# Second block of a two-block forward pass: four units direct and 18 pairs in place of six and 17, with another order of the first pair's residues

## The chip, the cores and the metric

One core of a Trainium2 chip runs the whole kernel as one program. The metric is the device time of one execution in microseconds (us); lower is better. The kernel is written by engine: TensorE (matmuls), VectorE (DVE), ScalarE (ACT), GpSimd (POOL) and SyncE (SP, which issues loads) each run their own list of instructions in order and meet only at semaphores.

## The reference, cut to what matters

Two transformer-like blocks follow each other on one sequence of 1024 tokens of width 1024, in fp32. The first is gated linear attention with a short convolution and a gated feed-forward part. The second, in which the change lies, begins with one wide projection:

```python
h = rmsnorm_2(x, g_norm[layer])
proj = h @ w_in[layer]           # 1024 -> 9 * 1024 columns
a_u, a_v, a_gate, q, k, v, b_gate, gate_logits = jnp.split(proj, splits, axis=-1)
y_a = chunked_spatial_gating(gelu(a_u), gelu(a_v), w_s, b_s, g_v) * silu(a_gate)
y_b = dilated_attention(q, k, v) * silu(b_gate)
g_a, g_b = jnp.split(sigmoid(gate_logits), 2, axis=-1)
merged = g_a * (y_a @ w_proj_a) + g_b * (y_b @ w_proj_b)
x = x + merged @ w_out
```

The columns of q, k, v (24 tiles of 128), a_v (8 tiles) and a_u (8 tiles) are the 40 units that the change deals with.

## The kernel before, in words

**Units.** A unit is a tile of 128 output columns for all 1024 tokens, with 1024 inputs in 8 parts of 128. The sums are kept near fp32: weights and activations are each split into a high part that TensorE takes as it is and a low part, the residue, and three matmuls (high by high, low by high, high by low) are added up (lines 839 to 841). A direct unit is 2 halves of tokens x 8 parts x 3 = 48 matmuls of 512 columns. For each unit SP loads 512 KB of raw weights (line 513), ScalarE casts them to the high part (line 1289), GpSimd makes the residue in two instructions (line 727), TensorE multiplies, and VectorE takes the result out of PSUM (line 1941).

**Pairs.** Two units together are a 2 x 2 by 2 x 2 product of blocks (inputs in even and odd parts, tokens in left and right halves). `pair_of_units` computes it with seven block products instead of eight, by Winograd's form of Strassen's rule. One block product is `times`: 4 parts x 3 matmuls = 12 matmuls, so a pair is 84 matmuls where two direct units are 96. Each product needs its weights as a high part in a ring of four half buffers (`hi_half` on ScalarE, line 1455) and the residue of it (`lo_half` on GpSimd, line 767). Four of the seven weight blocks are sums (`weight_sums` on VectorE, lines 2151 to 2162). After a pair, VectorE and ScalarE join the four PSUM banks into two tiles; three VectorE additions (lines 2349 to 2354 in the second block) stand between product 3 and product 6. `half(p, i)` says which half buffer product i of pair p uses; at one pair the ring skips a buffer, so that it ends where the next stage needs it.

**Opening of the second block.** Products 0, 1 and 3 read sums of activations (x_sums_split), products 2, 4, 5 and 6 the four quarters of the activations themselves. Sums and quarters need their own high parts (`hi_sum`, `hi_again` on ScalarE, lines 1436 and 1443) and residues (`lo_sum`, `lo_again` on VectorE, lines 2131 and 2138). The quarters must be made anew, since the direct units read another scaling of the same buffer; their high parts can be written only when the last direct unit has been multiplied. All of this, eight scalings of the residual by VectorE (line 2306) and three differences (lines 2310 to 2323) happen while TensorE computes the six direct units 101 to 106 (`U_W` on). Then come the 17 pairs: q = 0 and 5 to 12 hold q, k, v tiles, 1 to 4 hold a_v, 13 to 16 hold a_u. Beside pairs 6 to 13 TensorE also transposes and mixes one a_v tile (group 0 to 7).

**What sets the order.** Nothing plans it at run time: each engine's list is written out by hand. The lines that matter are the end of the ScalarE list before the loop over q (lines 1632 to 1656), the VectorE list from `direct(0)` (line 2303) to the same loop, and `load_duo` on SP (line 545, its loads at 556), whose waits say when a raw buffer is free. There are two raw buffers for pairs: `WR`, which the direct units also use, and `WRB`, used by pairs alone (`w_pair`).

## Time and profile before

| what | value |
|---|---|
| median of 3 runs | 2347.03 us (2346.66 to 2348.51) |
| the profiled execution's own time | 2345.13 us |
| its span, first to last instruction | 2343.1 us |
| TensorE busy | 2330.0 us, 99% |
| VectorE, ScalarE, GpSimd busy | 56%, 37%, 35% |
| granted TensorE clock, mean | 0.999 |

The span is the stretch of the trace; the own time of the profiled execution is 2.0 us longer, since it also holds what lies around the first and the last instruction. All times inside the kernel are counted from the start of the span. A busy share of 99% on one engine says that the others matter only where they make it wait. In a timeline row the number after the start is the duration; instructions of one kind that follow each other closely are merged, with their count (x2) and their total.

### The profile page before, as it was taken

What the parts mean: (1) busy time and instruction counts of PE and PEld (TensorE: products, weight loads), DVE (VectorE), ACT (ScalarE), POOL (GpSimd) and SP (SyncE); (2) the same over time, 40 slices, a digit from 0 to 9 for tenths busy, and PEclk for the clock granted to TensorE, in tenths of its full rate; (3) what the DMA queues carried; (4) which work ended last, traced back from release to release, by engine and by line L of the source; (5) the groups of instructions that cost most, each with busy time, mean ns of one, the idle gap of its engine ahead of it and who ended that gap; (6) DMA issues with size and microseconds to landing.
All of it is one profiled execution on the core that took longest, in us unless ns stands there. A gap on an engine that the chain in (4) does not pass through costs nothing.

```text
span 2343.1 us, 30043 instructions
## 1 busy us (share of the span) xinstructions
PE 2330.0 (99%) x11126; PEld 1939.0 (83%) x11126; DVE 1316.8 (56%) x1830; ACT 867.8 (37%) x1309; POOL 822.2 (35%) x543
## 2 busy tenths in 40 slices
PE   9999999999999999999999999999999999999998
PEld 7888888888888888888888888888888888888887
DVE  6445764864444432247745445678787787752445
ACT  5422323233323331133443223455555555541122
POOL 3322222355555533322555455312222222223332
PEclk9999999999999999999999999999999999999999
DMA  3111222232222252223312323432332332353223
GB/s 144 43 42 37 98 82 99 81 153 81 81 81 81 81 177 93 81 99 119 116 67 74 113 98 122 156 109 91 106 125 91 97 116 81 108 189 126 108 99 117
DMA packets 70448, 238.02 MB, mean 102 GB/s; under 512 B 8432, under 2 KB 12752, under 8 KB 70224
## 3 DMA queue, kind: packets, MB, share of 16 engines
q1 hardware_dynamic: 54416, 181.20, 23.2%
q10 hardware_dynamic: 15936, 55.49, 5.9%
q8 instruction: 66, 1.08, 0.2%
q14 instruction: 30, 0.25, 0.0%
HBM read 177.41 MB, written 59.24 MB: 101 GB/s over the span
## 4 chain that ended last, share of the span: by engine, by line
PE 98%; DVE 1%; DMA 0%; issue 0%; ACT 0%; SPq 0%; DVEq 0%; ACTq 0%
PE dense L839 19%; PE dense L841 18%; PE dense L840 18%; PE dense L1030 10%; PE dense L1032 10%; PE dense L1031 10%; PE aux L1169 3%; PE aux L1182 2%; PE aux L1154 1%; PE aux L1181 1%; PE aux L1153 1%; PE aux L1116 1%; PE aux L984 1%; PE aux L863 0%; PE aux L955 0%; PE dense L1253 0%
## 5 line engine op out<-in xcount | busy, mean ns | idle before, releaser
L727 POOL TENSOR_TENSOR w_lo<-w_raw,w_hi 128x512 fp32r<-128x512 f32 x246 | 387.5, 1596 | 982.2 <-ACT w_hi L1289 973.1
L839 PE MATMUL dense<-x_hi,w_hi 128*128 128x512 f32 x1424 | 578.6, 406 | 0.4 <-DVE x_lo L1887 0.4
L841 PE MATMUL dense<-x_hi,w_lo 128*128 128x512 f32 x1424 | 557.1, 391 | 0.0
L840 PE MATMUL dense<-x_lo,w_hi 128*128 128x512 f32 x1424 | 556.7, 391 | 0.0
L1289 ACT CAST w_hi<-w_raw 128x1024 fp32r<-128x1024 f32 x121 | 127.1, 1051 | 539.8 <-PE dense L841 523.9
L841 PEld LDWEIGHTS dense<-x_hi,w_lo 128*128 128x128 f32 x1424 | 267.5, 188 | 57.7
L767 POOL TENSOR_TENSOR w_lo<-w_sums,w_hi 128x512 fp32r<-128x512 f32 x144 | 228.9, 1598 | 229.5 <-ACT w_hi L1455 229.4
L839 PEld LDWEIGHTS dense<-x_hi,w_hi 128*128 128x128 f32 x1424 | 268.2, 188 | 45.7 <-issue 1.2
L840 PEld LDWEIGHTS dense<-x_lo,w_hi 128*128 128x128 f32 x1424 | 268.7, 189 | 43.3
L1030 PE MATMUL dense<-x_hi,w_hi 128*128 128x512 f32 x576 | 226.0, 392 | 1.1 <-DVE work L2217 0.9
L1031 PE MATMUL dense<-x_lo,w_hi 128*128 128x512 f32 x576 | 224.5, 390 | 0.0
L1032 PE MATMUL dense<-x_hi,w_lo 128*128 128x512 f32 x576 | 224.5, 390 | 0.0
L1455 ACT CAST w_hi<-w_sums 128x512 fp32r<-128x512 f32 x144 | 89.1, 620 | 238.8 <-DVE w_sums L2151 169.4
L1030 PE MATMUL dense<-x_sums_split,w_hi 128*128 128x512 f32 x432 | 168.4, 390 | 0.0
L1032 PE MATMUL dense<-x_sums_split,w_lo 128*128 128x512 f32 x432 | 168.4, 390 | 0.0
L1031 PE MATMUL dense<-x_sums_split,w_hi 128*128 128x512 f32 x432 | 168.3, 390 | 0.0
L1721 ACT CAST att_p_hi<-aux 128x512 fp32r<-128x512 f32 x192 | 92.0, 479 | 144.7 <-PE aux L1169 144.4
L839 PE MATMUL dense<-work_split,w_hi 128*128 128x512 f32 x352 | 137.4, 390 | 0.7 <-DVE work_split L2167 0.6
L840 PE MATMUL dense<-work_split,w_hi 128*128 128x512 f32 x352 | 137.2, 390 | 0.0
L841 PE MATMUL dense<-work_split,w_lo 128*128 128x512 f32 x352 | 137.1, 390 | 0.0
L2422 DVE TENSOR_TENSOR att_p_lo<-aux,att_p_hi 128x512 fp32r<-128x512 f32 x192 | 106.2, 553 | 50.8 <-ACT att_p_hi L1721 50.0
L2109 DVE TENSOR_TENSOR residual<-dense,residual 128x1024 f32<-128x1024 f32 x32 | 39.2, 1224 | 167.5 <-PE dense L841 167.5
(301 smaller groups left out, 3934.5 us busy)
## 6 DMA issues: line engine op xcount, KB each, us to landing
w_raw<-weights SPq DMA_DIRECT2D x163, 512.0 KB, 3.8
w_raw_b<-weights SPq DMA_DIRECT2D x34, 512.0 KB, 4.2
kept_qkv<-work ACTq DMA_DIRECT2D x24, 512.0 KB, 2.9
kept_m<-work ACTq DMA_DIRECT2D x22, 512.0 KB, 2.7
work<-kept_m SPq DMA_DIRECT2D x22, 512.0 KB, 3.3
residual<-xT SPq DMA_DIRECT2D x16, 512.0 KB, 6.5
kept_x<-residual ACTq DMA_DIRECT2D x16, 512.0 KB, 2.6
att_q<-kept_qkv SPq DMA_DIRECT2D x32, 256.0 KB, 4.0
```

The source lines that it names most:

```text
L727: last = pool.tensor_tensor(WL[:, u.slot, at4], WR[:, u.slot, at4], WH[:, u.slot, at4].bitcast(f32), ALU.subtract)
L767: pool.tensor_tensor(WL[:, h // 2, at4], quarter(p, i), WH[:, h // 2, at4].bitcast(f32), ALU.subtract).then_inc(*((d_lo, 1) if i < 6 else ...
L839: pe.matmul(dst, WH[:, u.slot, k], hi, start=(k == 0), stop=False)
L840: pe.matmul(dst, WH[:, u.slot, k], lo, start=False, stop=False)
L841: last = pe.matmul(dst, WL[:, u.slot, k], hi, start=False, stop=(k == nk - 1))
L1030: pe.matmul(bank(b), wh, hi[:, j], start=(first and j == 0), stop=False, skip_group_check=True)
L1031: pe.matmul(bank(b), wh, lo[:, j], start=False, stop=False, skip_group_check=True)
L1032: last = pe.matmul(bank(b), wl, hi[:, j], start=False, stop=(j == 3), skip_group_check=True)
L1289: act.copy(WH[:, u.slot], WR[:, u.slot]).then_inc(w_hi, 1)
L1455: act.copy(WH[:, h // 2, 4 * (h % 2):4 * (h % 2) + 4], quarter(p, i)).then_inc(*((d_hi, 1) if i < 6 else (w_hi, 2)))
L1721: act.copy(PH[:, k % 2, lo:HALF], PA[:, bank, lo:HALF]).then_inc(ph, 1)
L2422: dve.tensor_tensor(PL[:, k % 2, lo:HALF], PA[:, bank, lo:HALF], PH[:, k % 2, lo:HALF].bitcast(f32), ALU.subtract).then_inc(pl, 1)
```

## The change

The second block computes four units directly and 18 pairs. The tiles of q, k and v take pairs 0 and 5 to 13, those of a_u pairs 14 to 17. The skips of the ring of half buffers are at pairs 6 and 12 instead of pair 8. The first pair of the second block reads its raw weights from `WRB`, the second from `WR`, and so on in turn, so SP issues the first pair's load behind the load of the last direct unit, and the second pair's when the last direct unit's residue is made. On ScalarE the first two casts of the first pair stand ahead of the third sum's, the left quarters' casts don't wait for the third difference, and the copy of the first product waits for the third sum's residue. On VectorE the first pair's weight sums come ahead of the third direct tile; the residues follow as second sum, first quarter, third sum, second quarter, third quarter, fourth quarter; the second pair's first two weight sums come behind the fourth quarter's residue, inside the loop.

```diff
-U_W, V_DIRECT, V_DUOS = 101, 6, 17
+U_W, V_DIRECT, V_DUOS = 101, 4, 18
...
 def is_au(q):
-    return q >= 13
+    return q >= 14
...
-    return 16 * (V_DIRECT // 2 + (q > 0) + min(max(q - 5, 0), 8))
+    return 16 * (V_DIRECT // 2 + (q > 0) + min(max(q - 5, 0), 9))
...
         def half(p, i):
-            return (7 * own(p) + i + 2 + (min(p // 4, 3) if p < DUOS else min(own(p) // 8, 1))) % 4
+            return (7 * own(p) + i + 2 + (min(p // 4, 3) if p < DUOS else min(own(p) // 6, 2))) % 4
...
         def w_pair(p):
-            return WRB if own(p) % 2 else WR
+            return WRB if own(p) % 2 == (p < DUOS) else WR
...
             def load_duo(p):
-                if own(p) == 0:
-                    sp.wait_ge(w_lo, units_before(p))
+                if p in (0, DUOS + 1):
+                    sp.wait_ge(w_lo, units_before(p - own(p)))
                 elif p == 1:
                     sp.wait_ge(mm_done, U_OUT + KT)
-                elif own(p) == 1:
+                elif p == DUOS:
                     sp.wait_ge(m_ready, TILES)
...
             def hi_again(e, t, p=0):
                 act.wait_ge(mm_done, units_before(p))
-                act.wait_ge(t_sum, 4 if p < DUOS else 8)
+                if p < DUOS or t:
+                    act.wait_ge(t_sum, 4 if p < DUOS else 8)
...
             hi_sum(1, XV[:, 0, :, HALF:S], 4)
-            split(Unit(U_W + 4))
-            keep(2)
+            hi_half(p, 0)
+            hi_half(p, 1)
             act.wait_ge(sp_r1, 16)
             hi_sum(2, XSUM[:], 4)
-            split(Unit(U_W + 5))
-            keep(3)
-            hi_half(p, 0)
-            hi_half(p, 1)
-            keep(4)
+            keep(2)
+            hi_again(0, 0, p)
             hi_half(p, 2)
-            hi_again(0, 0, p)
             hi_half(p, 3)
             hi_again(1, 0, p)
...
                 if q == 0:
-                    keep(5)
+                    keep(3)
                     hi_again(0, 1, p)
...
                 else:
+                    act.wait_ge(t_lo, 6)
                     keep_p1(p)
                     hi_half(p, 5)
                     hi_again(1, 1, p)
...
             lo_sum(0, XSUM[:], 3)
-            direct(2)
             dve.wait_ge(t_lo, 4)
             dve.wait_ge(t_sum, 6)
             dve.tensor_tensor(XSUM[:], b22, b12, ALU.subtract).then_inc(t_sum, 1)
+            weight_sums(DUOS)
+            direct(2)
             lo_sum(1, b12, 3)
-            direct(3)
             dve.wait_ge(t_lo, 5)
             dve.wait_ge(t_sum, 7)
             dve.tensor_tensor(b12, b21, XSUM[:], ALU.subtract).then_inc(t_sum, 1)
+            direct(3)
+            lo_again(4, 0, 0)
             lo_sum(2, XSUM[:], 3)
-            direct(4)
-            weight_sums(DUOS)
-            weight_sums(DUOS + 1, 0)
-            direct(5)
-            lo_again(4, 0, 0)
             lo_again(5, 1, 0)
             lo_again(6, 0, 1)
...
                 if q == 0:
                     lo_again(7, 1, 1)
+                    weight_sums(p + 1, 0)
```

## Rows read from the trace of the kernel before

**Rows 1.** The page: busy time by engine, and the chain that ended last

```profile
PE 2330.0 (99%) x11126; PEld 1939.0 (83%) x11126; DVE 1316.8 (56%) x1830; ACT 867.8 (37%) x1309; POOL 822.2 (35%) x543
...
PE 98%; DVE 1%; DMA 0%; issue 0%; ACT 0%; SPq 0%; DVEq 0%; ACTq 0%
```

**Rows 2.** TensorE's waits over the whole span, by line and releaser

```profile
PE dense L897 <- DVE x_lo L1887: 1.2, 1, 1.2
...
PE dense L1030 <- DVE work L2217: 0.9, 1, 0.9
...
PE dense L1030 <- issue: 0.2, 1, 0.2
```

**Rows 3.** Stretches: busy us (count) by engine, clock, DMA share, GB/s

```profile
1077.00:1148.20 71.20, 71.20 (x330) 59.27 (x329) 54.88 (x44) 18.79 (x18) 22.59 (x12) 1.00 0.31 119
1148.20:1167.25 19.05, 19.05 (x85) 15.77 (x84) 15.69 (x12) 14.16 (x16) 14.51 (x8) 1.00 0.23 83
```

**Rows 4.** Timeline of TensorE: start, duration, instruction

```profile
1148.21 0.39 PE L1030 MATMUL dense<-x_sums_split,w_hi 128*128 128x512 f32 x1
...
1153.65 0.39 PE L1030 MATMUL dense<-x_hi,w_hi 128*128 128x512 f32 x1
...
1167.25 0.39 PE L1030 MATMUL dense<-x_sums_split,w_hi 128*128 128x512 f32 x1
```

**Rows 5.** Timeline of VectorE, idle time and releaser in brackets

```profile
1118.18 2.28 DVE L2131 TENSOR_TENSOR x_sums_split<-x_sum,x_sums_split 128x2048 fp32r<-128x2048 f32 x1
...
1121.51 3.16 DVE L2318 TENSOR_TENSOR x_sum<-residual 128x2048 f32<-128x2048 f32 x1
1124.59 3.39 DVE L2131 TENSOR_TENSOR x_sums_split<-residual,x_sums_split 128x2048 fp32r<-128x2048 f32 x1
...
1137.60 1.22 DVE L1941 TENSOR_TENSOR work<-dense,rstd 128x1024 f32<-128x1024 f32 x1 [2.99 <-PE dense L841]
1138.74 0.68 DVE L2151 TENSOR_TENSOR w_sums<-w_raw 128x512 f32<-128x512 f32 x1
...
1140.79 1.66 DVE L2162 TENSOR_TENSOR w_sums<-w_raw,w_sums 128x512 f32<-128x512 f32 x1
...
1148.48 1.22 DVE L1941 TENSOR_TENSOR work<-dense,rstd 128x1024 f32<-128x1024 f32 x1 [3.50 <-PE dense L841]
1150.02 2.61 DVE L2138 TENSOR_TENSOR x_lo<-residual,x_hi 128x1024 fp32r<-128x1024 f32 x2 [0.31 <-ACT x_hi L1443]
...
1159.29 0.69 DVE L2349 TENSOR_TENSOR p_p<-p_p,dense 128x512 f32<-128x512 f32 x1
...
1161.41 2.52 DVE L2138 TENSOR_TENSOR x_lo<-residual,x_hi 128x2048 fp32r<-128x2048 f32 x1
...
1166.92 1.67 DVE L2162 TENSOR_TENSOR w_sums<-w_raw_b,w_sums 128x512 f32<-128x512 f32 x1
```

**Rows 6.** Timeline of GpSimd

```profile
1078.62 2.56 POOL L727 TENSOR_TENSOR w_lo<-w_raw,w_hi 128x512 fp32r<-128x512 f32 x2 [5.60 <-ACT w_hi L1289]
...
1121.23 4.60 POOL L727 TENSOR_TENSOR w_lo<-w_raw,w_hi 128x512 fp32r<-128x512 f32 x2 [9.72 <-ACT w_hi L1289]
...
1140.21 3.38 POOL L767 TENSOR_TENSOR w_lo<-w_sums,w_hi 128x512 fp32r<-128x512 f32 x2 [7.75 <-ACT w_hi L1455]
```

**Rows 7.** Timeline of ScalarE

```profile
1139.51 1.22 ACT L1455 CAST w_hi<-w_sums 128x512 fp32r<-128x512 f32 x2 [11.75 <-DVE w_sums L2151]
...
1148.94 2.00 ACT L1443 CAST x_hi<-residual 128x1024 fp32r<-128x1024 f32 x2
```

**Rows 8.** Timeline of SyncE's queue

```profile
1056.72 55.15 SPq L513 DMA_DIRECT2D w_raw<-weights  x6
1132.49 0.80 SPq L556 DMA_DIRECT2D w_raw<-weights  x2
```

**Rows 9.** TensorE's last matmuls (timeline), and a later microsecond, columns as in rows 3

```profile
2334.43 0.60 PE L1237 MATMUL aux<-work,ones 128*128 128x256 f32 x2
...
2338.00:2339.00 1.00, 0.00 (x0) 0.00 (x0) 0.14 (x1) 0.00 (x0) 0.00 (x0) 0.55 1.04 339
```

More of the change, by code:

```diff
@@ L102, in au_tile @@
 def au_tile(q):
-    return 2 * (q - 13)
+    return 2 * (q - 14)
 def qkv_tile(q):
@@ L1592, in left_half @@
                     act.wait_ge(sp_t[0], 16 * 12)
-                    if q > 13:
+                    if q > 14:
                         act.wait_ge(mx_upd, au_tile(q))
```

## The prediction, made before the result was known

> **What bounds the kernel now.** I read the page first. TensorE is busy for 99% of the span and is 98% of the chain that ended last; no other engine is above 56% [rows 1]. So a microsecond is lost or won only where TensorE issues less or waits more. The waits of TensorE come next: in the whole span they are seven, 1.2, 1.1, 0.9, 0.6, 0.4, 0.4 and 0.2 us, of which the first and the two of a pair's line stand in [rows 2]. Those two (0.9 and 0.2 us, line 1030) are in the opening of the first block's pairs, where VectorE was late; in the second block's pairs TensorE never waits. Then the stretches around the change: in the direct units (1077.0 to 1148.2) and in the first pair (to 1167.25) TensorE is busy without a break, at a granted clock of 1.00, while VectorE is busy for 54.88 of 71.20 us, then for 15.69 of 19.05 [rows 3]. That last share is the warning: the opening has little room on VectorE. The timeline gives the prices: a product of the pair is 12 matmuls; product 0 starts at 1148.21, product 2 at 1153.65, the next pair at 1167.25 [rows 4]. That is 2.72 us a product, 0.2267 us a matmul (the duration of 0.39 us in the row is pipelined), 19.04 us a pair of 84 matmuls.
>
> **What is removed.** Two direct units go and one pair comes. A direct unit is 48 matmuls, 10.88 us; the two last evacuations by VectorE, 1137.60 and 1148.48, are 10.88 us apart too [rows 5]. So TensorE issues 96 matmuls less and 84 more: 21.76 - 19.04 = 2.72 us saved. This is the largest gain possible; nothing else in the second block's pairs is waiting [rows 2].
>
> **What the opening has to do in less time.** The four direct units now end at 1148.21 - 21.76 = 1126.45. Until then VectorE must have made the sums of the right and left halves, their residues, the first pair's weight sums and the direct tiles. VectorE's start is not earlier: its eight scalings come first, and up to the residue of the first sum (1118.18, 2.28 long, so to 1120.46) nothing in its order changes [rows 5]. From there I put its new order together from the durations of before:
> - second difference: 2.28 us, 1120.5 to 1122.8. The row shows 3.16 because GpSimd was splitting at 1121.23 [rows 5, 6], a split that now is gone.
> - four weight sums of the first pair: before, 1138.74 to 1142.45, the last one 1.66 us long since GpSimd's first half split (1140.21) stood beside it. Same pattern: 1122.7 to 1126.4. Evacuation of the third direct tile starts 1.6 after the last sum starts: 1126.3 to 1127.5. Product 0 waits for it (its banks are those of that tile): start 1127.6, **1.15 us late**. Its weights are there: ScalarE's cast starts 0.77 after the first sum, GpSimd's residue follows 0.7 later and takes about 1.6 (before: 1138.74, 1139.51, 1140.21) [rows 5 to 7], so about 1125.9.
> - residue of the second sum to 1129.75, third difference to 1132.05, evacuation of the last direct tile to 1133.2. Product 1 (1130.3 to 1133.05) is on time.
> - residue of the first quarter, two instructions, 2.61 less 0.38 of waiting = 2.2 us [rows 5], from 1133.15. Between its two parts GpSimd gets one half split in. Price of that: the two engines take turns when both operands of VectorE are in SBUF. At 1121.23 GpSimd's two splits took 4.60 us while VectorE ran its 3.16, and not the 2.56 of an undisturbed two at 1078.62; VectorE's residue of 1124.59 took 3.39 and not 2.28 [rows 5, 6]. So each split that falls in costs VectorE about 1.1 us. The Trainium skill, SBUF — State Buffer, "Who interferes with whom", says that such a pair of instructions blocks one another wholly, whichever was first; a rule against this change, which packs VectorE and GpSimd closer. Residue ready at 1136.55, product 2 there and not at 1133.05: **3.5 us late**; it ends at 1139.35.
> - residue of the third sum, one more split before it: 1137.7 to 1139.95. Product 3 at 1140.0, **0.65 late**, ends 1142.75.
> - residue of the second quarter to 1142.15; product 4 on time, to 1145.45.
> - residue of the third quarter after one split, to 1145.45; then the three additions (before, from 1159.29, with 1161.41 for what follows [rows 5]), the second done about 1.5 us after the start of the first: 1146.95. Product 5 **1.5 late**, to 1149.65.
> - residue of the last quarter, from 1147.55 to 1149.8: product 6 **0.2 late**, to 1152.55.
> - the second pair: its first two weight sums now follow the last quarter, the right half of its first tile leaves at 1155.4, product 1 was due at 1155.25: **0.2 late**.
>
> The sum of the waits is 1.15 + 3.5 + 0.65 + 1.5 + 0.2 + 0.2 = 7.2 us. The same reckoning, done for the six-unit opening, comes out 0.9 us too late: it gives GpSimd the turn twice where the trace gives it to VectorE (1150.02, two parts in 2.61, and 1161.41 in 2.52 [rows 5]). I take 0.2 off and keep 7.0. Net: 7.0 - 2.72 = **+4.3 us**.
>
> Ends of the unknown, the number of splits that VectorE must let pass: none gives 7.0 - 3.3 = 3.7 us of waits, net +1.0; five instead of three gives 7.0 + 2.3, net +6.6. Three is nearest to the rows: in the opening of before some rows carry such a wait and others hardly any (1161.41: 2.52 for 2.28; 1166.92: 1.67 where a sum takes 0.68) [rows 5].
>
> **Edits that cost nothing.** The first pair's weights go to the other raw buffer and are issued behind the load of the fourth unit. The last six loads of units were issued from 1056.72 to 1111.87, each behind a residue two units earlier; the fourth unit's goes out near 1081, so the pair's are there 30 us before 1122.7, where before they went out at 1132.49 [rows 8]. The second pair's go out at 1111.6, earlier too. Two residues and casts of whole units fall away on GpSimd and ScalarE: off the path. ScalarE's casts of the left quarters no longer wait for the third difference; they start at 1128.0, when the third tile's store is issued, and need 2.0 us [rows 7], 3 us before VectorE comes to them. Its new wait for the third residue (1140.0) stands before the copy of the first product: behind it wait two casts, product 4 needs the copy at 1142.75, it is there at 1140.6. The skips in the ring of half buffers move from pair 8 to pairs 6 and 12; such a skip leaves three products (8.2 us) for a cast of 0.62 and a residue of 1.3 to 1.7 us, and at pair 8 TensorE did not wait [rows 2]. The last four pairs (the ones that gate the mixed tiles) move one place back, with more slack; the hand-over to attention keeps its order. If one of these covers fails it would be a wait of 1 us or so in a stretch that has none now.
>
> **Rivals.**
> 1. TensorE is covered: VectorE keeps up, only 2.72 us go away, 2344.3. For it: the new order serves products in the order of their need, and VectorE was idle for 2.99 and 3.50 us ahead of the evacuations of 1137.60 and 1148.48 [rows 5]. Against it: two fewer units take 21.76 us from the front, two evacuations and two weight sums free only 3.7 us, and the eight scalings stay. 0.03.
> 2. VectorE and GpSimd hardly meet: +1.0 to +2.5, about 2349. 0.10.
> 3. Clearly slower: the gap before product 2 lowers TensorE's clock. In the trace TensorE's last matmuls ended at 2335.0, and the granted clock was 0.55 in the microsecond from 2338, so it was at its lower level, 1.2 GHz, for most of it [rows 9]. It fell 3 us after the last matmul, and the gap here is 3.4 us. Deciding point: whether it falls before product 2 begins. Then product 2 takes 5.4 instead of 2.7 us. One slow product is mostly hidden by VectorE's chain (product 3's residue is ready at 1140.0, it would start at 1142.0, then product 5 again waits on VectorE): +0.4. Two slow products end at 1147.5 and cost 3.1: +7.4 net, 2354.4. The Trainium skill, TensorE: Matmul & The Clock Gate, "Why this matters for your kernels", warns of idle gaps between bursts of matmuls. The first opening's 0.9 us gap left the clock alone. 0.15.
> 4. The change is neutral in some other way or hits a stall I did not see in the later pairs: 0.04, spread both ways.
>
> **From cases to numbers.** The forecast (net +4.3, its own range +3 to +6) has 0.68. The profiled execution took 2345.13 us (span 2343.1); the forecast for it is 2349.4. The median of the runs is 2347.03, 1.9 above the profiled one; the predicted time is 2347.03 + 4.3 = 2351.3. A measurement of this kernel tells 0.2%, 4.7 us, from no change; the forecast lies just inside. Of its 0.68 I put 0.39 inside and 0.29 outside; rival 1, 2 and half of 4 inside (0.15), rival 3 nearly all outside (0.14 of 0.15), half of 4 outside (0.02). Same 0.54, slower 0.45; faster by over 4.7 us would need more than the 2.72 us that exist: 0.01. Range: 2348.6 (waits of 4.3 us) to 2354.6 (five splits, or two slow products), which leaves out rival 1 and the tails.
>
> **What would show it.** Right: 12 matmuls fewer; TensorE waits on VectorE before products 0, 2, 3 and 5 of the second block's first pair, the longest before product 2; VectorE without idle time from 1097.8 to 1150; residues of 3.4 us beside GpSimd's splits. Wrong: no wait there (rival 1); a granted clock under 1.00 near 1137 (rival 3); a wait at pairs 6 or 12, or a wait for GpSimd's residue of the weights at product 0.

## The result, and the profile after

The changed kernel takes 2351.82 us (median of 19 executions; a 20th, at 10295 us, is set aside as an outlier, and with it the median is 2352.10), the kernel before 2347.38 us in executions taken beside it (20). The ratio is 1.0019, interval 1.0013 to 1.0025: **+0.19%, some 4.4 us slower**, with 3.1 and 5.9 us as the ends of the interval. It is just inside the 0.2% that was set as the bound of no change; the predicted time was 2351.3 us, and the measured one lies in the range given.

The profiled execution of after took 2354.96 us (span 2352.4), 9.8 us more than the one of before, so not all of what its trace shows is the change; this is sorted out below. Its page:

```profile
PE 2332.9 (99%) x11114; PEld 1938.8 (82%) x11114; DVE 1317.8 (56%) x1837; ACT 870.9 (37%) x1316; POOL 823.6 (35%) x546
...
PE 96%; DVE 2%; DMA 1%; issue 0%; ACT 0%; SPq 0%; DVEq 0%; ACTq 0%
```

11,114 matmuls are 12 fewer than in [rows 1], as the edit wants. In the chain TensorE has lost two points to others. The waits of TensorE over the whole span say which (line and releaser; us in total, times, longest):

```profile
PE dense L1030 <- DVE x_lo L2136: 3.3, 1, 3.3
PE dense L839 <- DVE work_split L2165: 2.5, 1, 2.5
...
PE dense L1030 <- DVE work L1939: 1.0, 1, 1.0
```

In [rows 2] TensorE never waited in the second block's pairs. Now it does, twice for VectorE: 1.0 us for the evacuation of the third direct tile (line 1939), 3.3 us for a quarter's residue (line 2136). The timeline of TensorE gives the places (start, duration, instruction; in brackets the idle time and who ended it):

```profile
1131.39 0.39 PE L841 MATMUL dense<-x_hi,w_lo 128*128 128x512 f32 x1
1132.78 0.50 PE L1030 MATMUL dense<-x_sums_split,w_hi 128*128 128x512 f32 x1 [1.00 <-DVE work L1939]
...
1141.83 0.47 PE L1030 MATMUL dense<-x_hi,w_hi 128*128 128x512 f32 x1 [3.28 <-DVE x_lo L2136]
...
1145.95 0.63 PE L1030 MATMUL dense<-x_sums_split,w_hi 128*128 128x512 f32 x1
...
1151.72 0.39 PE L1030 MATMUL dense<-x_hi,w_hi 128*128 128x512 f32 x1
...
1176.20 0.39 PE L1030 MATMUL dense<-x_sums_split,w_hi 128*128 128x512 f32 x1
```

The first row is the last matmul of the direct units; it ends (at the spacing of 0.227 us) at 1131.62. Product 0 starts at 1132.78, product 2 at 1141.83, product 3 at 1145.95, product 5 at 1151.72, and the third pair at 1176.20. Two pairs need 38.08 us (2 x 19.04), so the opening has lost 1176.20 - 1131.62 - 38.08 = **6.50 us**, and with the 2.72 us saved it is **+3.78 us**. How this is spread, from the starts of the products: 1.16 before product 0, 0.17 before product 1, 3.44 before product 2, 1.40 before product 3, 0.33 before product 4, and nothing after. The parts before products 3 and 4 are no waits: from 1143.39 seven matmuls of product 2 follow each other at 0.43 us and not at 0.23, TensorE's lower level of 1.2 GHz, and product 3 begins in the same stretch. The windows show it (columns as in [rows 3]; the clock is the third number from the end):

```profile
1090.00:1096.00 6.00, 6.00 (x24) 4.91 (x24) 4.59 (x11) 1.02 (x3) 0.00 (x0) 0.72 0.07 29
1096.00:1127.00 31.00, 31.00 (x138) 25.57 (x137) 25.53 (x16) 7.87 (x6) 7.43 (x4) 1.00 0.31 119
1127.00:1137.00 10.00, 9.00 (x40) 7.11 (x39) 9.90 (x8) 6.90 (x8) 4.65 (x3) 1.00 0.13 52
1140.00:1145.00 5.00, 3.17 (x10) 2.60 (x11) 5.00 (x3) 1.72 (x1) 2.88 (x2) 0.82 0.11 43
1145.00:1150.00 5.00, 5.00 (x20) 4.03 (x20) 5.00 (x4) 3.44 (x4) 2.57 (x1) 0.84 0.00 0
```

VectorE is busy for 9.90 of 10 us and then for the whole of 5 and 5 us, and TensorE waits for it before products 0 and 2. VectorE's timeline:

```profile
1104.06 13.71 DVE L2304 SCALAR_TENSOR_TENSOR residual<-residual,gain_product,rstd 128x1024 f32<-128x1024 f32 x8
...
1123.34 2.29 DVE L2129 TENSOR_TENSOR x_sums_split<-x_sum,x_sums_split 128x2048 fp32r<-128x2048 f32 x1
1125.66 2.29 DVE L2315 TENSOR_TENSOR x_sum<-residual 128x2048 f32<-128x2048 f32 x1
...
1129.92 1.68 DVE L2160 TENSOR_TENSOR w_sums<-w_raw_b,w_sums 128x512 f32<-128x512 f32 x1
1131.51 1.21 DVE L1939 TENSOR_TENSOR work<-dense,rstd 128x1024 f32<-128x1024 f32 x1
...
1138.31 3.43 DVE L2136 TENSOR_TENSOR x_lo<-residual,x_hi 128x1024 fp32r<-128x1024 f32 x2
1141.66 3.37 DVE L2129 TENSOR_TENSOR x_sums_split<-x_sum,x_sums_split 128x2048 fp32r<-128x2048 f32 x1
1144.95 4.48 DVE L2136 TENSOR_TENSOR x_lo<-residual,x_hi 128x2048 fp32r<-128x2048 f32 x2
...
1150.13 0.69 DVE L2347 TENSOR_TENSOR work<-p_p,dense 128x512 f32<-128x512 f32 x1
```

The second difference (1125.66) takes 2.29 us and no longer the 3.16 of [rows 5]; the sum of 1129.92 takes 1.68, the first quarter's residue 3.43, the third sum's 3.37, where 2.2 to 2.3 is undisturbed. The last row is the second addition, which product 5 waits for: it is done at 1150.82, and product 5 starts at 1151.72, right behind product 4. So at product 5 TensorE, still late from its low clock, is behind VectorE by 0.9 us. Beside the first quarter's and the third sum's residue stand GpSimd's splits of the pair's weights:

```profile
1103.92 3.52 POOL L727 TENSOR_TENSOR w_lo<-w_raw,w_hi 128x512 fp32r<-128x512 f32 x2 [19.22 <-ACT w_hi L1289]
1112.78 3.90 POOL L727 TENSOR_TENSOR w_lo<-w_raw,w_hi 128x512 fp32r<-128x512 f32 x2 [5.34 <-ACT w_hi L1289]
...
1138.38 2.27 POOL L767 TENSOR_TENSOR w_lo<-w_sums,w_hi 128x512 fp32r<-128x512 f32 x1
1140.60 2.27 POOL L767 TENSOR_TENSOR w_lo<-w_raw_b,w_hi 128x512 fp32r<-128x512 f32 x1
1147.43 3.16 POOL L767 TENSOR_TENSOR w_lo<-w_raw_b,w_hi 128x512 fp32r<-128x512 f32 x1 [4.55 <-ACT w_hi L1456]
```

One instruction of GpSimd that takes 1.3 us alone lasts 2.27 here, and the residue beside it lasts 1.1 longer. Such a hold-up of VectorE by one instruction of GpSimd is called a turn below. Note the first two rows: two whole-unit splits (four instructions) lie beside the eight scalings (1104.06, 13.71 us). The view of that one line gives the scalings singly, as shortest, median and longest in ns:

```profile
L2304 DVE SCALAR_TENSOR_TENSOR residual<-residual,gain_product,rstd x8: 1271/1754/2307, 1104.1 to 1115.5; 128x1024 f32<-128x1024 f32 x8
```

The same instruction on tiles of one shape takes 1.27 us or 2.31 us. The prediction had passed over this; experiments below take it up.

**Where the 9.3 us of span go.** Opening, +3.78. At the hand-over to the first block's down projection TensorE waits 2.5 us for a tile (line 839, second wait above) and then runs at the lower level for a while: +3.4 together, in code that the change does not touch. Around 1090 to 1095, after the token sums, the clock is 0.72 in the first window above, where before had 1.00 throughout [rows 3]: +1.65. The start, the rest of the pairs and the end make the remaining 0.5. Whether the second and third of these belong to the change is the first question of the experiments.

### The profile page after: what moved, and what is told of

It reads as the page before. It is cut to its first block, busy times and chain, and to the rows that moved or that the text cites. A ratio compares the mean times of both kernels' runs of the same rounds, so it can differ in the third digit from the quotient of the medians.

```text
span 2352.4 us, 30048 instructions
## 1 busy us (share of the span) xinstructions
PE 2332.9 (99%) x11114; PEld 1938.8 (82%) x11114; DVE 1317.8 (56%) x1837; ACT 870.9 (37%) x1316; POOL 823.6 (35%) x546
## 4 chain that ended last, share of the span: by engine, by line
PE 96%; DVE 2%; DMA 1%; issue 0%; ACT 0%; SPq 0%; DVEq 0%; ACTq 0%
PE dense L839 18%; PE dense L841 18%; PE dense L840 18%; PE dense L1030 10%; PE dense L1032 10%; PE dense L1031 10%; PE aux L1169 3%; PE aux L1182 1%; PE aux L1154 1%; PE aux L1181 1%; PE aux L1153 1%; PE aux L1116 1%; PE aux L984 1%; DVE residual L2304 1%; DVE x_lo L2136 0%
## 5 line engine op out<-in xcount | busy, mean ns | idle before, releaser
L727 POOL TENSOR_TENSOR w_lo<-w_raw,w_hi 128x512 fp32r<-128x512 f32 x242 | 377.3, 1581 | 976.9 <-ACT w_hi L1289 967.5
L767 POOL TENSOR_TENSOR w_lo<-w_sums,w_hi 128x512 fp32r<-128x512 f32 x148 | 234.1, 1590 | 243.2 <-ACT w_hi L1456 243.2
L841 PEld LDWEIGHTS dense<-x_hi,w_lo 128*128 128x128 f32 x1392 | 261.7, 188 | 56.7
L839 PEld LDWEIGHTS dense<-x_hi,w_hi 128*128 128x128 f32 x1392 | 262.2, 188 | 45.1 <-issue 1.5
L840 PEld LDWEIGHTS dense<-x_lo,w_hi 128*128 128x128 f32 x1392 | 262.9, 189 | 42.5
L1030 PE MATMUL dense<-x_sums_split,w_hi 128*128 128x512 f32 x444 | 173.2, 390 | 1.0 <-DVE work L1939 1.0
L1031 PE MATMUL dense<-x_sums_split,w_hi 128*128 128x512 f32 x444 | 172.9, 389 | 0.0
```

The lines of the kernel that those rows point to most:

```text
L727: last = pool.tensor_tensor(WL[:, u.slot, at4], WR[:, u.slot, at4], WH[:, u.slot, at4].bitcast(f32), ALU.subtract)
L767: pool.tensor_tensor(WL[:, h // 2, at4], quarter(p, i), WH[:, h // 2, at4].bitcast(f32), ALU.subtract).then_inc(*((d_lo, 1) if i < 6 else ...
L839: pe.matmul(dst, WH[:, u.slot, k], hi, start=(k == 0), stop=False)
L840: pe.matmul(dst, WH[:, u.slot, k], lo, start=False, stop=False)
L841: last = pe.matmul(dst, WL[:, u.slot, k], hi, start=False, stop=(k == nk - 1))
L1030: pe.matmul(bank(b), wh, hi[:, j], start=(first and j == 0), stop=False, skip_group_check=True)
```

## The experiments

"Lost" below is the measure just used: start of the third pair, less the end of the direct units, less 38.08 us; it is 0.00 before and 6.50 in after. Kernels with four units have 2.72 us to set against it. The shares by product are all read from the starts of the products' first matmuls. Medians are given with that of before in executions beside them.

| kernel | lost | before product 0 | 1 | 2 | 3 | 4 | 5 | rest |
|---|---|---|---|---|---|---|---|---|
| after | 6.50 | 1.16 | 0.17 | 3.44 | 1.40 | 0.33 | 0.00 | 0.00 |
| after, again | 6.49 | 1.16 | 0.18 | 3.43 | 1.31 | 0.41 | 0.00 | 0.00 |
| small splits | 3.97 | 1.15 | 0.14 | 2.40 | 0.12 | 0.00 | 0.00 | 0.16 |
| one more difference, four units | 9.50 | 3.45 | 1.69 | 1.93 | 0.53 | 0.14 | 1.32 | 0.44 |
| filler | 7.24 | 1.15 | 0.14 | 3.50 | 0.53 | 0.13 | 1.33 | 0.46 |
| old sequence | 11.57 | 9.10 | 2.45 | 0.02 | 0.00 | 0.00 | 0.00 | 0.00 |
| gain on ScalarE | 6.24 | 0.91 | 0.13 | 3.47 | 1.54 | 0.19 | 0.00 | 0.00 |
| the same, reordered | 6.10 | 0.00 | 0.26 | 4.08 | 1.72 | 0.04 | 0.00 | 0.00 |
| early split | 3.75 | 0.00 | 0.00 | 2.06 | 1.69 | 0.00 | 0.00 | 0.00 |
| scale from PSUM | 4.22 | 0.00 | 0.00 | 0.70 | 0.53 | 0.62 | 1.92 | 0.45 |
| the same, reordered | 2.10 | 0.00 | 0.00 | 0.00 | 0.14 | 0.58 | 0.73 | 0.65 |
| and a later cast | 2.12 | 0.00 | 0.00 | 0.00 | 0.15 | 0.58 | 0.72 | 0.67 |

### The changed kernel once more

No edit.

> The changed kernel once more, unaltered, for a second trace. Theory: the waits in the opening stay within 0.7 us of 6.5 (they follow from the instruction lists), while the stretches of TensorE at half clock outside the opening (near 850 and 1092 us, 3.2 us lost together) differ from execution to execution and may be absent; the net of the opening is +3.8 to +4.6 us. Rival: the low clock near 1092 and the longer wait near 849 belong to the change and are there again.

2351.56 us against 2348.39: 1.0016 (1.0006 to 1.0025). The opening repeats to 0.1 us in every entry of the table. The wait at the down projection is 0.6 us in this trace, as long as in the trace of before, so the 3.4 us there are an accident of one execution. The two low-clock stretches come back; the windows of this kernel, which runs 3 to 4 us earlier:

```profile
1086.00:1092.00 6.00, 6.00 (x25) 5.02 (x25) 4.20 (x11) 1.42 (x3) 0.00 (x0) 0.72 0.09 37
1137.00:1142.00 5.00, 3.81 (x12) 3.10 (x13) 5.00 (x3) 1.08 (x1) 2.23 (x2) 0.76 0.00 0
```

In after they were at 1090 to 1095 and 1143 to 1146. The second belongs to the opening. On the first, the traces of the experiments speak: the stretch from the token sums (32 matmuls of one column each, which come just before it) to the end of the direct units is 43.01 us in before (two units of 10.88 us each taken off) and in one other of the 14 traces (the last but one kernel below); in the remaining 12 it is longer by 1.6 or 3.2 us, with six units (below) as well as with four. It does not come from the change; it makes some of the spread of the single times, and it is why two traces differ by more than two medians.

### GpSimd's part made small

```diff
-                pool.tensor_tensor(WL[:, h // 2, at4], quarter(p, i), WH[:, h // 2, at4].bitcast(f32),
+                n = 8 if p == DUOS and i >= 2 else P
+                pool.tensor_tensor(WL[:, h // 2, at4, 0:n], quarter(p, i)[:, :, 0:n],
+                                   WH[:, h // 2, at4, 0:n].bitcast(f32),
```

> The changed kernel, but GpSimd makes only 8 of 128 columns of the residue of the weights for products 2 to 6 of the second block's first pair (the rest of those residues stays old: this part of the computation is left out). TensorE's waits in the first two pairs of the second block were 6.5 us in the trace of the changed kernel. Theory (VectorE's list is the bound there and each residue on GpSimd that falls between its instructions holds it up by about 1.1 us): VectorE's residues take 2.2 to 2.3 us each, the wait before product 2 shrinks from 3.4 to about 2.3 us, and the waits together to 3.5 to 4 us; the kernel about 2.5 us faster than the changed one. Rival (GpSimd is not in VectorE's way): the waits stay at 6.5 us. Rival (products wait for the weights' residues): the first wait, before product 0, goes away as well.

2350.15 us against 2348.39: 1.0009 (1.0000 to 1.0018). Lost: 3.97 us, 2.5 less than after. VectorE's timeline of this kernel:

```profile
1137.09 2.34 DVE L2130 TENSOR_TENSOR x_sums_split<-x_sum,x_sums_split 128x2048 fp32r<-128x2048 f32 x1
1139.36 4.48 DVE L2137 TENSOR_TENSOR x_lo<-residual,x_hi 128x2048 fp32r<-128x2048 f32 x2
```

The third sum's residue takes 2.34 us and not 3.37, the first quarter's 2.35 and not 3.43. So VectorE is freed of two turns, at 1.05 us each. Product 2 comes 1.04 earlier, which is one of them. Product 3 comes another 1.28 earlier, and there two things go at once: the second turn, and the low clock, for the clock stays up in this trace. How much of the 2.5 us each of them is, this run does not part; in after product 5 started 0.9 us behind the addition that it needs, so about 0.9 was the clock and about 1.6 the turns. Of product 2's lateness, 2.4 us remain without them: VectorE's own work.

### One more difference for VectorE, with four units and with six

```diff
             dve.wait_ge(x_sc, KT)
+            chain(dve.tensor_tensor(XSUM[:], b22, b11, ALU.subtract))
             dve.tensor_tensor(XSUM[:], b22, b12, ALU.subtract).then_inc(t_sum, 1)
```

> The changed kernel with one more VectorE difference of 128x2048 (2.3 us) ahead of the first sum. Theory (VectorE is the bound from its scalings to the last quarter): all of it appears, TensorE's waits in the opening grow from 6.5 to about 8.7 us, almost all before product 0. Rival (the wait comes from ScalarE's order, GpSimd or a load): less than 1 us of it appears.

2354.23 us against 2348.39: 1.0025 (1.0015 to 1.0035). The wait before product 0:

```profile
PE dense L1030 <- DVE work L1939: 3.3, 1, 3.3
```

It was 1.0. Product 0 comes 2.29 us later for 2.29 us more of VectorE, one for one. By product 2 the sum is 7.07 against 4.77 in after, 2.30 again; at the end it is 3.0, the last 0.7 from a turn of GpSimd more (the second and third quarter take 5.58 us together, not 4.48), which the expectation, at 8.7 us, did not have.

The same instruction in the kernel before, behind the third sum's residue:

```diff
             lo_sum(2, XSUM[:], 3)
+            dve.wait_ge(t_lo, 6)
+            chain(dve.tensor_tensor(XSUM[:], b22, b11, ALU.subtract))
             direct(4)
```

> The kernel before (six direct units) with the same additional VectorE difference (2.3 us), behind the third sum's residue, where VectorE was idle for 2.99 us. Theory: TensorE waits no longer than in the kernel before, 0.0 us in the opening, same time within 0.5 us. Rival (VectorE was the bound before as well): up to 2.2 us slower.

2347.77 us against 2348.39: 0.9999 (0.9990 to 1.0008). Nothing is lost in the opening. VectorE's timeline of this kernel:

```profile
1138.38 2.29 DVE L2326 TENSOR_TENSOR x_sum<-residual 128x2048 f32<-128x2048 f32 x1
1141.37 1.23 DVE L1941 TENSOR_TENSOR work<-dense,rstd 128x1024 f32<-128x1024 f32 x1 [0.69 <-PE dense L841]
```

The idle time of 2.99 us that stood ahead of this evacuation [rows 5] has shrunk to 0.69, by the 2.3 us put in. With six units VectorE's list has slack; with four it has none, and that is the change's price. (With six units the low clock after the token sums was there too: its granted clock was 0.54 from 1088 to 1094.)

### TensorE kept busy through the gap

Twelve matmuls into a PSUM bank that is free at that point, between products 1 and 2.

```diff
                 times(p, 1, TX[:, 1, 0], TX[:, 1, 1], B5, True)
+                if p == DUOS:
+                    for _ in range(12):
+                        pe.matmul(PA[:, 3], TX[:, 0, 0, 0, 0:P], TX[:, 0, 0, 0], start=True, stop=True)
```

> The changed kernel; between products 1 and 2 of the second block's first pair TensorE issues 12 matmuls of 512 columns into an unused PSUM bank (2.72 us of the 3.4 us that it waits there). In both traces of the changed kernel TensorE ran at half clock for 7 or 8 matmuls behind this wait (1.4 to 1.6 us of their time). Theory (the low clock follows from the idle gap, but VectorE's chain hides it): product 2 starts as before, no matmul of the opening is slow, the waits of the first two pairs together stay at 6.3 to 6.7 us, since TensorE now waits before product 5 instead; the time is the same within 1 us. Rival (the low clock is what the opening costs on top): the opening gets 1.4 us or more shorter and the kernel faster by as much.

2352.56 us against 2347.47: 1.0024 (1.0015 to 1.0034). Windows of this kernel over the whole opening, then VectorE's timeline:

```profile
1125.00:1140.00 15.00, 13.38 (x58) 10.44 (x58) 14.90 (x11) 11.60 (x11) 10.55 (x5) 1.00 0.17 70
1140.00:1150.00 10.00, 8.59 (x37) 6.46 (x36) 9.86 (x7) 3.44 (x4) 5.18 (x2) 1.00 0.30 105
```

```profile
1141.59 5.59 DVE L2139 TENSOR_TENSOR x_lo<-residual,x_hi 128x2048 fp32r<-128x2048 f32 x2
```

The clock stays at its upper level, product 2 starts at the same place, and 7.24 us are lost instead of 6.50, above the 6.3 to 6.7 expected. What the clock gave back (1.40 becomes 0.53 before product 3) is paid before product 5, where TensorE now waits 1.2 us for VectorE's second addition (the 1.33 of the table). That addition is done 20.3 us behind the direct units, and in after it was 19.2, because GpSimd has one more turn (5.59 and not 4.48), as in the run with one more difference: ScalarE's copy of product 2's bank waits for product 2 and for the third sum's residue. In after it started at 1146.24, right behind the slow product 2 (14.6 us behind the direct units), in this run at 1141.70 (13.5 us behind them), and the cast and the split behind it came sooner with it. So the low clock was not hidden by VectorE's list as it stood in after, where 0.9 us of it showed; but keeping the clock up moved a turn of GpSimd into that list, and won nothing. The Trainium skill, TensorE: Matmul & The Clock Gate, "Why this matters for your kernels", advises against idle gaps between bursts of matmuls; the trace of after agrees, for the clock fell behind a gap of 3.28 us. The run shows that filling the gap did not pay here.

### The sequence of before, with four units

```diff
             lo_sum(0, XSUM[:], 3)
+            direct(2)
             ...
-            weight_sums(DUOS)
-            direct(2)
             lo_sum(1, b12, 3)
+            direct(3)
             ...
-            direct(3)
-            lo_again(4, 0, 0)
             lo_sum(2, XSUM[:], 3)
+            weight_sums(DUOS)
+            lo_again(4, 0, 0)
```

and on ScalarE the first two casts of the pair behind the third sum's.

> Four direct units and 18 pairs, but VectorE and ScalarE keep the sequence of the kernel before: the weight sums behind the third sum's residue, the sums' residues all ahead of the quarters', ScalarE's casts of the weights behind the third sum. Theory (VectorE's sum of work is the bound, the order only decides where the wait shows): product 0 starts 8 to 9 us late and nearly nothing is waited for afterwards; 8 to 9.5 us of waits together, so the new order is worth 1.5 to 3 us. Rival (the order is worth nothing, only the count matters): 6.5 us. Rival (the order is what makes it slower): under 6 us.

2358.18 us against 2347.47: 1.0046 (1.0032 to 1.0059), so 10.7 us slower than before. The wait before product 0, and windows of this kernel:

```profile
PE dense L1030 <- POOL w_lo L767: 8.9, 1, 8.9
```

```profile
1133.00:1135.00 2.00, 0.00 (x0) 0.00 (x0) 2.00 (x3) 0.45 (x1) 0.00 (x0) 0.50 0.00 0
1135.00:1140.00 5.00, 2.94 (x7) 2.40 (x8) 4.93 (x5) 5.00 (x7) 4.76 (x3) 0.50 0.00 0
```

Product 0 is late by 9.10 us, since its weight sum stands behind three sums' residues; by then most of the list is done, and no later product waits. The other 2.45 us are the low clock: it is down before product 0 starts, and product 0's twelve matmuls follow each other at about 0.43 us. 11.57 against 6.50 us: beside the old sequence the new one is worth 5.1 us, of which up to 2.45 is that clock; 1.5 to 3 us were expected, without it. The shorter direct part with the old sequence costs 8.85 us net. The two parts of the change pull in opposite directions, and the first is the larger.

### VectorE's scalings made lighter by arithmetic

The eight scalings multiply by a gain and by the reciprocal root in one instruction. ScalarE is asked to do the gain.

```diff
+            def gained(k):
+                act.wait_ge(x_ready, 24 + k + 1)
+                act.activation(XR[:, k], XR[:, k], ACT.Copy, scale=GG[:, k:k + 1]).then_inc(x_gain, 1)
...
-                dve.scalar_tensor_tensor(XR[:, k], XR[:, k], GG[:, k:k + 1], R[:], ALU.mult, ALU.mult
-                                         ).then_inc(x_sc, 1)
+                dve.wait_ge(x_gain, n + 1)
+                dve.tensor_tensor(XR[:, k], XR[:, k], R[:], ALU.mult).then_inc(x_sc, 1)
```

> The changed kernel; ScalarE, idle at that time, multiplies the eight tiles of the residual by the gain, so VectorE's eight scalings become plain products (1.15 us each by the rows of other products of 1024 columns, not 1.71): 4.5 us less on VectorE ahead of the first sum. Theory: product 0 is on time, the waits of the first two pairs fall from 6.5 to 2.6 to 3.6 us; the kernel is 3 to 4 us faster than the changed one, within 1 us of the kernel before. Rival (the waits come from anything behind the last direct unit, the high parts or GpSimd): the wait before product 0 goes, the others stay, 5.3 us.

2352.86 us against 2347.47: 1.0022 (1.0013 to 1.0031), and 6.24 us lost: a miss. VectorE's timeline of this kernel, and the line's own view:

```profile
1100.58 13.46 DVE L2316 TENSOR_TENSOR residual<-residual,rstd 128x1024 f32<-128x1024 f32 x8
```

```profile
L2316 DVE TENSOR_TENSOR residual<-residual,rstd x8: 1212/1723/2312, 1100.6 to 1111.7; 128x1024 f32<-128x1024 f32 x8
```

The plain product takes 1.21 us where the other took 1.27, but 2.31 in the longest, as before. The expectation had taken the mean of the eight (1.7 us) for the price of the operation. What costs the time is the neighbour: GpSimd's four instructions of that stretch, as two runs further down show.

The second run of this pair also puts the weight sums and the third tile ahead of the second difference, and the fourth tile behind the first quarter's residue.

```diff
             lo_sum(0, XSUM[:], 3)
+            weight_sums(DUOS)
+            direct(2)
             ...
-            weight_sums(DUOS)
-            direct(2)
             lo_sum(1, b12, 3)
             ...
-            direct(3)
             lo_again(4, 0, 0)
+            direct(3)
```

> As the kernel with the gain on ScalarE, and VectorE's first weight sums and third tile ahead of the second difference, the first quarter's residue ahead of the fourth tile. Theory: with VectorE 4.5 us ahead these can move up; product 2 is on time and product 5 the only one that waits more than 1 us; waits of 1 to 2.4 us together, so 0.3 to 1.7 us faster than the kernel before, less than the times can tell. Rival: GpSimd's residues of the weights become the bound, waits as in the kernel with the gain on ScalarE alone, about 3 us.

2352.70 us against 2347.47: 1.0019 (1.0010 to 1.0028), 6.10 us lost, the second miss, for the same reason. Product 0 is on time now; all of it comes back before product 2 (4.08), which waits 3.8 us for the fourth tile behind the quarter's residue (line 1950).

### GpSimd's turns taken out of the scalings

Two ways that leave the arithmetic alone. First, ScalarE casts the third unit ahead of its copies of the reciprocal root, so that GpSimd splits it before the scalings begin.

```diff
             root(4)
+            split(Unit(U_W + 2))
             rstd(3, WK[:, 9])
             ...
-            split(Unit(U_W + 2))
             keep(0)
```

> The changed kernel; ScalarE casts the third direct unit's weights ahead of the two copies of the reciprocal root instead of behind them, so that GpSimd's two residues of that unit are over before VectorE's eight scalings begin. In the trace of the changed kernel these scalings took 1.27 us each undisturbed and 2.31 us where one of GpSimd's four residues came between, 13.7 us together; with the plain products they took 13.5 us, so it is GpSimd and not their arithmetic. Theory: two of four turns go, the scalings take about 11.6 us, VectorE's chain is 2.1 us earlier, the wait before product 0 is gone and the waits of the first two pairs fall from 6.5 to 4.1 to 4.9 us. Rival (the scalings are slow by themselves): 13.5 us again, and 6.5 us of waits.

2349.30 us against 2347.09: 1.0010 (1.0001 to 1.0019). VectorE's timeline of this kernel:

```profile
1102.14 10.68 DVE L2304 SCALAR_TENSOR_TENSOR residual<-residual,gain_product,rstd 128x1024 f32<-128x1024 f32 x8
```

3.03 us less than 13.71, and 3.75 us lost in the opening instead of 6.50. That is better than expected (11.6 us and 4.1 to 4.9), since three turns went and not two: only one of the eight scalings still takes 2.31 us, and GpSimd's split of the fourth unit (1109.32, 4.65 us) lasts beyond their end at 1112.82. Of the 3.75 us, 1.69 stand before product 3, behind another fall of the clock. Second, the scalings read the reciprocal root from the two PSUM banks where TensorE left it, not from the copy in SBUF.

```diff
-                dve.scalar_tensor_tensor(XR[:, k], XR[:, k], GG[:, k:k + 1], R[:], ALU.mult, ALU.mult
+                dve.scalar_tensor_tensor(XR[:, k], XR[:, k], GG[:, k:k + 1], one(PA[:, 2:4]), ALU.mult, ALU.mult
```

> The changed kernel; the eight scalings read the reciprocal root from PSUM, where TensorE left it, and not from its copy in SBUF, so that each has one operand in SBUF only. Theory: GpSimd no longer comes between, the eight take 9.7 us instead of 13.7, GpSimd's residues beside them take 2.6 us a unit and not 3.5 to 3.9; VectorE's chain is 4 us earlier, and the waits of the first two pairs fall from 6.5 to 2.4 to 3.4 us. Rival (the turns don't depend on where the operand lies): 13.7 and 6.5 us.

2350.55 us against 2347.09: 1.0013 (1.0004 to 1.0022). The line's own view, and GpSimd's timeline:

```profile
L2304 DVE SCALAR_TENSOR_TENSOR residual<-residual,gain_product,aux x8: 1273/1276/1276, 1100.8 to 1109.2; 128x1024 f32<-128x1024 f32 x8
```

```profile
1100.68 2.54 POOL L727 TENSOR_TENSOR w_lo<-w_raw,w_hi 128x512 fp32r<-128x512 f32 x2 [19.21 <-ACT w_hi L1289]
1108.02 2.54 POOL L727 TENSOR_TENSOR w_lo<-w_raw,w_hi 128x512 fp32r<-128x512 f32 x2 [4.80 <-ACT w_hi L1289]
```

All eight now take 1.27 us, beside GpSimd's split of 1100.68, which itself takes 2.54 and not 3.52; together 9.61 instead of 13.71 us. One operand moved, no instruction fewer: four turns of GpSimd at 1.03 us. This is what the Trainium skill, SBUF — State Buffer, "Who interferes with whom", says: an instruction of VectorE with two inputs in SBUF contends with a GpSimd instruction that reads SBUF; one with at most one input there does not, outside VectorE's two-port modes. The traces agree in both halves (2.31 against 1.27 us beside GpSimd). Yet 4.22 us are still lost, above the 2.4 to 3.4 expected: with the list earlier, two more of GpSimd's half splits fall beside the quarters' residues (6.67 us for the second and third, where two undisturbed take 4.5), and product 5 waits 1.6 us for VectorE's second addition.

### Both, and in a better sequence

The last kernel with the reordering shown above for the second gain run.

> As the kernel that scales from PSUM, and with VectorE's weight sums and third tile ahead of the second difference and the first quarter's residue ahead of the fourth tile. Theory: the waits fall further, to 1.8 to 2.8 us together, so that the opening is even with or up to 0.9 us better than the kernel before; in the whole time the same as before within 1.5 us. Rival (no order helps, VectorE's sum of work decides alone): as the kernel that scales from PSUM.

2347.01 us against 2347.09: 0.9998 (0.9989 to 1.0007). The last direct matmul and product 0, from TensorE's timeline, then the two waits left in the opening, before products 5 and 4:

```profile
1126.58 0.39 PE L841 MATMUL dense<-x_hi,w_lo 128*128 128x512 f32 x1
1126.81 0.39 PE L1030 MATMUL dense<-x_sums_split,w_hi 128*128 128x512 f32 x1
```

```profile
PE dense L1030 <- DVE work L2347: 0.4, 1, 0.4
...
PE dense L1030 <- POOL w_lo L767: 0.3, 1, 0.3
```

No gap between units and pair; 2.10 us lost, so 0.6 us better than before in the opening. It is the best version found. Its execution time is even with before; 0.6 us is less than this comparison can tell.

The second wait is for GpSimd itself: product 4 needs the residue of its weights, whose making the turns stretch as well (two instructions in 6.64 us). What is left of turns is two beside the second and third quarter. One more kernel moves a cast of ScalarE back, so that the split behind it comes later.

```diff
                     keep_p1(p)
-                    hi_half(p, 5)
                     hi_again(1, 1, p)
+                    hi_half(p, 5)
```

> As the reordered kernel that scales from PSUM, and ScalarE casts the first pair's sixth half buffer of weights behind the last quarter's high part and not ahead of it. In the reordered kernel the second and third quarters' residues on VectorE took 6.7 us together, with two of GpSimd's residues between them and behind them, where they take 4.5 us undisturbed. Theory: one of the two turns moves beside VectorE's additions from PSUM, where it costs nothing; the two residues take about 5.6 us, the wait before product 5 shrinks by about 0.7 us, and the waits of the first two pairs fall from 2.1 to 1.2 to 1.6 us; 1 to 1.5 us less than the kernel before in this stretch, too little for the times to tell. Rival (the last quarter is late instead, or product 5 waits for its weights): 2.1 us or more again.

2347.49 us against 2347.55: 0.9999 (0.9990 to 1.0008), 2.12 us lost: no gain. GpSimd's timeline:

```profile
1141.50 3.07 POOL L767 TENSOR_TENSOR w_lo<-w_raw_b,w_hi 128x512 fp32r<-128x512 f32 x1 [0.23 <-ACT w_hi L1456]
```

VectorE's two residues run from 1136.73 for 6.69 us, to 1143.42. The split had to wait only 0.23 us for the later cast, so it still gets its turn before VectorE is through.

## Why the prediction was right, step by step

- **2.72 us saved, 12 matmuls fewer**: shown by the count (11,114 against 11,126). In no trace do the pairs behind the second lose anything to the moved skips of the ring or to the swapped raw buffers. The pairs' loads went out long before their use (weight sums from 1127.9 and 1153.9), from SyncE's timeline of after:

```profile
1085.09 0.91 SPq L556 DMA_DIRECT2D w_raw_b<-weights  x2
1116.71 0.81 SPq L556 DMA_DIRECT2D w_raw<-weights  x2
```

- **Product 0, predicted 1.15 late**: 1.16, for the tile it named. The longer VectorE list (one more difference) moved it one for one.
- **Product 2, 3.5 late after a total of 1.15**: it was put at 10.10 us behind the end of the direct units and stood at 10.21. That VectorE's list ends this wait is shown by the added difference, which came through whole. The price of a turn was put at 1.1; 1.05 was measured by making the splits small.
- **Product 3, 0.65, and product 5, 1.5**: waits on VectorE were forecast before both, and neither is in the trace. Product 3 lost 1.40 us and product 4 another 0.33 to the low clock, and product 5 nothing. The forecast had VectorE's second addition done 20.5 us behind the direct units; it was done 19.2 behind, since the turn in the third quarter's residue did not come, and product 5 started 20.1 behind, held by TensorE's own lateness. With the clock up (filler) the turn came and the addition was done at 20.3, nearly as forecast.
- **Product 6 and the second pair, 0.2 each**: nothing in after; 0.46 with the filler.
- **The sum, 7.0**: 6.50. Net +3.78 against +4.3. It came so close in part by luck: up to product 4 the trace lost 6.50 us where 5.3 were forecast, because of the clock, and behind it nothing where 1.9 were forecast, because of the missing turn. The median moved by 4.4 (3.1 to 5.9), which holds both; of the 0.7 between trace and median nothing is shown.
- **The profiled execution**: forecast 2349.4, it was 2354.96, of which 3.4 is a wait in the first block and 1.65 a low-clock stretch, neither of the change.
- **Rival 3, the clock**: the fall came, the sign that was named for this rival (0.82 in the window from 1140), but 1.5 us into product 2 and not before it, so seven matmuls were slow and not twelve or more. The case of one slow product put it at +0.4 with the rest hidden; 0.9 showed at product 5. **Rival 1** (covered) is out by the waits. **Rival 2** (engines hardly meet): beside the one in the fourth weight sum three turns were assumed; after has two on the way to product 5 (first quarter, third sum), the third quarter had none. With small splits the net is 3.97 - 2.72 = +1.25, close to the +1.0 reckoned for no turns.
- **What it did not see**: "its eight scalings come first", 13.7 us, was taken as fixed. 4.1 us of it were the same turns that it priced everywhere else. Before pays them too (13.71 us for the same eight), so the forecast did not suffer, but it is the remedy that it missed.

## What to carry to other kernels

A list that runs in the shadow of another engine has a price as soon as the shadow is shortened: before you take work off the bounding engine, add up what the others do in that stretch and find where they last sat idle. When instances of one instruction on one shape differ (1.27 and 2.31 us), look at the neighbour engine before the arithmetic; moving one operand to PSUM took 4.1 us off VectorE's list, where a whole 128x2048 difference is 2.3. A low granted clock costs what it shows at the next wait and not the sum of its slow matmuls; ask what that wait would be without it, and which transfers or splits a faster engine would bring forward. Here it showed 0.9 us beside a full VectorE list, and all of its 2.45 us where nothing waited behind it (old sequence).

## What the runs showed of the hardware

- A turn of GpSimd (a 128x512 fp32 instruction) cost VectorE 1.03 to 1.1 us where both operands of both lay in SBUF, and GpSimd's instruction grew from 1.3 to 2.3 us or more. It goes in between VectorE's instructions although VectorE's list had no gap, and even between the two parts of one residue.
- In after the clock did not fall in the gap: behind 3.28 us of waiting (what came before was TensorE busy at full clock), product 2 ran at 0.23 us a matmul for some 1.5 us (1141.83 on), then seven matmuls followed each other at 0.43, then 0.23 again. In the gap of 8.9 us of the old sequence it did fall (0.50 from 1133 to 1135, with TensorE idle). Behind a gap of 2.2 us (small splits) it did not fall, behind one of 1.9 us (early split) it did.
- Thirty-two matmuls of one column (3.7 us, counted as busy) were followed by a stretch at the lower level in 12 of 14 traces, at a cost of 1.6 or 3.2 us. What decides between these was not tried.
